# Branch attention with a turned output, a two-unit compressed branch, and two norms merged into one

## The chip, the cores and the metric

The kernel runs on one core of one Trainium2 chip. The metric is the device time of one execution in microseconds (us). Engines: TensorE (PE for its matmuls, PEld for its weight loads), VectorE (DVE), ScalarE (ACT), GpSimd (POOL) and SyncE (SP), which here only issues loads.

## What is computed

Two transformer blocks of two layers each run one after the other on 512 positions of width 1024, in float32. Shown is the second layer of the first block, which the change touches, and the seam to the second block:

```
def nsa_attention(x, norm_g, w_in, w_out, kv):       # 16 heads of 64, 2 key/value groups
    proj = rmsnorm(x, norm_g) @ w_in                  # queries, and a gate per head and branch
    ...
        s = einsum('bghqd,bgnd->bghqn', q_c, k_cmp) * scale          # compressed: 31 keys
        s = jnp.where(valid, s - slopes * dist, NEG)
        p_cmp = softmax(s) * valid.any(-1, keepdims=True)
        o_cmp = einsum('bghqn,bgnd->bghqd', p_cmp, v_cmp)
        ...                                           # o_slc and o_win: the same over the keys up to
        s = jnp.where(ok, s - slopes * dist, NEG)     # the query, with keys and values of their own
        o = g_c[0] * o_cmp + g_c[1] * o_slc + g_c[2] * o_win
    return out @ w_out
...
    return rmsnorm(h, final_norm)                     # end of the first block
    h = rms_norm(x, g_mix[layer])                     # first line of the second
```

With 512 positions the selection takes all 8 blocks and the window spans everything, so both large branches are plain causal attention with a slope per head.

## The kernel before

Activations lie with the width on partitions: `x` is 8 tiles of 128 x 512. A projection splits activations and weights into a high part (fp32r, a rounded float32) and a low rest and takes three fp32r matmuls per pair (`three`). Weights come as panels of 128 x 1024 through a ring of four slots: SP loads `raw`, ACT writes `wh`, DVE writes `wl` (`split_high`, `split_low`, `ahead`), four panels ahead of the matmuls. Results come into four PSUM banks, which DVE empties (`banks_freed`). Each engine runs its instructions in program order; `plan` lists the stages and each stage adds its part to every engine. Semaphores alone tie the engines together.

`Residual` adds a projection to `x`; behind each tile ACT and DVE make the next stage's `xh` and `xl`, and POOL adds the squares into `ssq`. `Norm` turns `ssq` into `rstd`: PE sums over partitions, ACT takes the root, DVE the reciprocal, PE spreads it, DVE copies it out. By default (`late`) PE does this between the panels of the next projection, since the factor is applied to its results; with `now=True` it does it first. At the seam of the blocks a `Norm(now=True)` is followed by `Prepare`, where DVE scales each tile of `x` by the norm and by `final_norm` (L334), ACT and DVE make `xh` and `xl`, and ACT and POOL sum the squares again for a second, late `Norm`.

The attention layer: `KeysValues`, `Project` (queries), `Gates`, `StackQueries` (high and low parts of the queries), `Compress` (the 31 compressed keys and values), `CompressedAttention`, `StackKeys` (keys stacked so that one matmul over 128 rows takes the query's high part against both parts of the key), `CausalAttention("sparse")`, `Split`, and `Residual("w_o")`.

`CompressedAttention` runs 8 units (2 groups x 4 query tiles), each on 128 x 256 scores of 8 heads, in a pipeline over PE (L1453 scores on 64-row tiles, L1462 turning, L1470 values), DVE and ACT, and writes `o` with positions on partitions. `StackKeys` starts when it is over.

`CausalAttention` runs 128 units: 8 head pairs x 2 heads x 2 branches x 4 query tiles. A unit is: two score matmuls of up to 512 columns (L1706, L1707), bias and maximum in one DVE instruction (L1805), exponential with row sum on ACT (L1763), up to four transposes (L1679), a copy to SBUF on ACT (L1752), up to four fp32 matmuls of 128 columns against the values of both groups (L1692), of which one group's 64 columns are used, and on DVE reciprocal, gate and a scaled addition to `o` (L1782, L1823, L1836). Per head ACT also stages bias and queries (L1723, L1731, L1733), `staged_low` with the other head's half set to zero. `Split` then turns `o` into `o_high` and `o_low`.

## Time and profile before

| | |
|---|---|
| median of 3 runs | 2863.46 us (2861.43 to 2864.09) |
| the profiled execution | 2863.38 us, its span 2861.6 us |
| PE / PEld busy | 94% / 77% |
| DVE / ACT / POOL busy | 50% / 35% / 9% |
| mean granted TensorE clock | 0.96 of full speed |

The profiled execution's own time is the span and 1.8 us around it. A matmul's record reaches to its modelled end and overlaps the next one's, so distances between starts tell what a matmul costs, not lengths. The view by stage is that of the busy times in windows.

### The profile page before, as it was taken

How to read it: one execution, taken by the hardware profiler on the slowest of the kernel's cores; microseconds unless marked ns; L12 is line 12 of the kernel's file. 1: busy time of each engine (PE TensorE's matmuls, PEld its weight loads, DVE VectorE, ACT ScalarE, POOL GpSimd, SP SyncE). 2: the span in 40 equal slices, each digit the busy share in tenths (PEclk: the TensorE clock that was granted, in tenths of full speed). 3: DMA queues.
4: the chain of work that ended last, by engine and by line, in shares of the span. 5: the costliest groups of instructions: out<-in, count | busy, mean ns of one | idle time of the engine just before them, and what ended most of it. 6: DMA issues, size and time to landing. Idle time of an engine off the chain costs nothing.

```text
span 2861.6 us, 36729 instructions
## 1 busy us (share of the span) xinstructions
PE 2680.3 (94%) x12628; PEld 2191.1 (77%) x12628; DVE 1438.7 (50%) x2530; ACT 997.2 (35%) x1739; POOL 266.1 (9%) x252
## 2 busy tenths in 40 slices
PE   6989999999788899999799899899999999899999
PEld 5857888878677788888668778688887877588887
DVE  6885444334656554443534455554433565454422
ACT  4544232222377633222232533332322123332321
POOL 2002000110000020002300040200001040200000
PEclk9999999999689999999899999899999998899999
DMA  4202333233200033332222013133322323033331
GB/s 147 67 0 69 101 95 93 80 106 122 70 1 1 0 95 96 95 90 81 86 75 89 1 59 103 30 103 95 93 87 95 104 89 103 30 103 95 93 98 67
DMA packets 61358, 222.45 MB, mean 78 GB/s; under 512 B 7232, under 2 KB 7488, under 8 KB 60624
## 3 DMA queue, kind: packets, MB, share of 16 engines
q1 hardware_dynamic: 58896, 209.15, 23.9%
q0 software_dynamic: 2368, 12.06, 1.3%
q8 instruction: 57, 0.93, 0.1%
q14 instruction: 37, 0.30, 0.0%
HBM read 216.47 MB, written 2.10 MB: 76 GB/s over the span
## 4 chain that ended last, share of the span: by engine, by line
PE 85%; DVE 8%; ACT 3%; issue 2%; DMA 0%; POOL 0%; ACTq 0%; DVEq 0%; SPq 0%; POOLq 0%
PE psum L208 24%; PE psum L209 24%; PE psum L210 24%; PE psum L1692 3%; DVE conv_out L754 2%; PE psum L1679 1%; DVE wl L191 1%; PE psum L1065 1%; PE psum L1117 1%; ACT wh L185 1%; PE psum L1706 1%; PE psum L1707 1%; DVE xl L344 1%; PE psum L1709 1%; PE psum L2313 1%
## 5 line engine op out<-in xcount | busy, mean ns | idle before, releaser
L208 PE MATMUL psum<-xh,wh 128*128 128x512 f32 x1880 | 744.9, 396 | 55.3 <-DVE wl L191 22.9
L209 PE MATMUL psum<-xl,wh 128*128 128x512 f32 x1880 | 739.4, 393 | 0.0
L210 PE MATMUL psum<-xh,wl 128*128 128x512 f32 x1880 | 738.8, 393 | 0.0
L185 ACT ACTIVATE wh<-raw 128x1024 fp32r<-128x1024 f32 x404 | 422.9, 1056 | 895.5 <-PE psum L210 893.1
L191 DVE TENSOR_TENSOR wl<-raw,wh 128x1024 fp32r<-128x1024 f32 x404 | 541.5, 1353 | 246.1 <-ACT wh L185 246.0
L208 PEld LDWEIGHTS psum<-xh,wh 128*128 128x128 f32 x1880 | 356.7, 190 | 139.1 <-issue 27.7
L210 PEld LDWEIGHTS psum<-xh,wl 128*128 128x128 f32 x1880 | 356.5, 190 | 76.4 <-issue 0.9
L209 PEld LDWEIGHTS psum<-xl,wh 128*128 128x128 f32 x1880 | 356.8, 190 | 74.4 <-issue 0.6
L208 PE MATMUL psum<-hidden_high,wh 128*128 128x512 f32 x704 | 278.4, 395 | 0.0
L210 PE MATMUL psum<-hidden_high,wl 128*128 128x512 f32 x704 | 278.0, 395 | 0.0
L209 PE MATMUL psum<-hidden_low,wh 128*128 128x512 f32 x704 | 277.9, 395 | 0.0
L611 POOL TENSOR_TENSOR square<-x 128x512 f32 (+1 forms) x72 | 85.6, 1189 | 1726.5 <-DVE x L650 1509.7
L650 DVE TENSOR_TENSOR x<-psum,x 128x512 f32 (+1 forms) x72 | 49.5, 688 | 324.6 <-PE psum L210 324.5
L503 DVE TENSOR_TENSOR up<-psum,rstd 128x512 f32<-128x512 f32 x96 | 66.3, 691 | 262.6 <-PE psum L210 262.6
L626 ACT ACTIVATE xh<-x,cols (+1 forms) x64 | 46.4, 724 | 363.3 <-DVE x L650 332.8
L208 PEld LDWEIGHTS psum<-hidden_high,wh 128*128 128x128 f32 x704 | 132.3, 188 | 33.7 <-DVE wl L191 2.2
L210 PEld LDWEIGHTS psum<-hidden_high,wl 128*128 128x128 f32 x704 | 132.3, 188 | 31.7
L209 PEld LDWEIGHTS psum<-hidden_low,wh 128*128 128x128 f32 x704 | 132.4, 188 | 31.0
L480 ACT ACTIVATE hidden_high<-up 128x512 f32 x88 | 55.6, 632 | 175.7 <-DVE up L514 175.7
L494 DVE TENSOR_TENSOR pre<-psum,rstd 128x512 f32<-128x512 f32 x96 | 66.3, 691 | 75.7 <-PE psum L210 74.6
L615 POOL TENSOR_TENSOR ssq<-ssq,square 128x512 f32<-128x512 f32 x72 | 103.6, 1438 | 8.0
L518 DVE TENSOR_TENSOR hidden_low<-up,hidden_high 128x512 f32 x88 | 60.9, 692 | 81.8 <-ACT hidden_high L480 81.8
(363 smaller groups left out, 3473.5 us busy)
## 6 DMA issues: line engine op xcount, KB each, us to landing
raw<-ffn_in SPq DMA_DIRECT2D x176, 512.0 KB, 3.5
raw<-ffn_out SPq DMA_DIRECT2D x64, 448.0 KB, 4.1
raw<-ffn_out SPq DMA_DIRECT2D x32, 512.0 KB, 3.6
raw<-pw SPq DMA_DIRECT2D x24, 512.0 KB, 3.6
raw<-o_w_hgg SPq DMA_DIRECT2D x12, 512.0 KB, 4.0
raw<-w_q SPq DMA_DIRECT2D x8, 512.0 KB, 4.3
raw<-w_o SPq DMA_DIRECT2D x8, 512.0 KB, 3.6
raw<-e_w_qk SPq DMA_DIRECT2D x8, 512.0 KB, 3.5
```

The source lines that it names most:

```text
L185: self.nc.scalar.activation(self.wh[:, slot, :], self.raw[:, slot, :], ACT.Copy).then_inc(self.weights_high.sem, 1)
L191: self.nc.vector.tensor_tensor(self.wl[:, slot, :], self.raw[:, slot, :], self.wh[:, slot, :].bitcast(F32), ALU.subtract).then_inc(self.we ...
L208: nc.tensor.matmul(out, ah, bh, start=start, stop=False)
L209: nc.tensor.matmul(out, ah, bl, start=False, stop=False)
L210: return nc.tensor.matmul(out, al, bh, start=False, stop=stop)
L494: dve.tensor_tensor(c.pre[:, r, :], c.psum[:, bank, :], c.rstd[:], ALU.mult).then_inc(c.banks_freed.sem, 1)
L503: dve.tensor_tensor(c.up[:, r, :], c.psum[:, bank, :], c.rstd[:], ALU.mult).then_inc(c.banks_freed.sem, 1)
L518: dve.tensor_tensor(self.hidden[1][:, at, :], c.up[:, r:r + 1, :], self.hidden[0][:, at, :].bitcast(F32), ALU.subtract).then_inc(self.read ...
L611: pool.tensor_tensor(c.square[:, m % 2, :].rearrange("p (a n) -> p a n", a=1), c.x[:, at, :], c.x[:, at, :], ALU.mult).then_inc(self.squar ...
L615: pool.tensor_tensor(c.ssq[:], c.ssq[:], c.square[:, m % 2, :], ALU.add).then_inc(self.summed.sem, 1)
L754: dve.scalar_tensor_tensor(out, taps, w, out, ALU.mult, ALU.add).then_inc(self.tapped.sem, 1)
L1692: mm = pe.matmul(c.psum[:, 1 + u % 2, 0:P], self.pt_sb[u % 4][:, t * P:(t + 1) * P], vals, start=(t == 0), stop=(t == i))
```

## The change

- `CompressedAttention` works in 2 units (one per group) of 128 x 1024: 16 score matmuls each, over all 128 rows against keys laid out in diagonal blocks (`kc` with a column range per half), 4 DVE and 1 ACT instructions over the whole unit, transposes into four banks. It makes no output: its turned probabilities stay as `pt`.
- `StackKeys` moves ahead of `Compress`; its second ACT part (`EvenKeys`) stands behind it.
- `BranchAttention` replaces `CausalAttention("sparse")` and `Split`. A round is one head and one branch with all four query tiles: 32 rounds. Scores: 8 matmuls, of which the four with `low` take only the head's 64 rows. No staging; POOL makes the bias of a head (`slope`). DVE multiplies the probabilities by gate over row sum, in place, in SBUF (L1860 of the changed kernel). Ten transposes fill three and a half banks, one per key tile; DVE copies the widest, ACT the other three. The values are the stationary operand (64 columns), the turned probabilities the moving one (512, 384, 256, 128 columns), and all products of a head pair, the compressed branch's first, add up in one bank that already has the width on partitions; ACT and DVE split it into `o_high` and `o_low` once per pair. `parts[1]` lies over the queries' low part.
- At the seam, `Residual("ffn_out1")` makes `xh` and `xl` with the product of both gains, ACT and POOL sum a second, weighted set of squares beside the first, and `DoubleNorm` works out both norms from them, late. `x` itself is scaled by DVE in `DoubleNorm.vector`, 8 instructions.

```diff
+class DoubleNorm(Norm):
+    def sums(self, pe):
+        pe.wait_ge(s.w_summed.sem, KD + 1)
+        for q, squares in enumerate((c.ssq, c.pre[:, 0, :])):
+            for i in range(NT):
+                mm = pe.matmul(c.psum[:, 5, q * NT + i:q * NT + i + 1], squares[:, i * P:(i + 1) * P],
...
+    def vector(self, dve):
...
+        dve.tensor_copy(c.rstd[:], c.psum[:, 4, :]).then_inc(self.done.sem, 1)
+        for m in range(KD):
+            c.nc.vector.scalar_tensor_tensor(c.x[:, m, :], c.x[:, m, :], c.col("final_norm", m),
+                                             c.psum[:, self.BANK, :], ALU.mult, ALU.mult).then_inc(self.scaled.sem, 1)
+        dve.wait_ge(self.done.sem, self.first + 6)
@@ Residual.gpsimd, Residual.scalar
+                if self.weighted:
+                    pool.wait_ge(self.w_squared.sem, m + 1 + self.body * i)
+                    pool.tensor_tensor(c.pre[:, 0, :], c.pre[:, 0, :], c.up[:, m % 2, :], ALU.add).then_inc(
+                        self.w_summed.sem, 1)
...
+                if self.weighted:
+                    after(act, self.w_summed, m + self.body * i)
+                    act.activation(c.up[:, m % 2, :].rearrange("p (a n) -> p a n", a=1), c.x[:, at, :], ACT.Square,
+                                   scale=c.col("final_norm", m + self.body * i)).then_inc(self.w_squared.sem, 1)
@@ CompressedAttention.tensor
+        for g in range(2):
+            for i in range(NT):
+                for h in range(4):
+                    at = 256 * (i % 2) + 64 * h
+                    mm = pe.matmul(c.psum[:, 2 * g + i // 2, at:at + 64], self.q[:, 4 * g + h, i * P:(i + 1) * P],
+                                   self.comp.kc[:, g, :], start=True, stop=True, skip_group_check=True)
+class BranchAttention(Stage):
+    ROUNDS, SETS, TURNED, RING, BIASES = 4 * KD, 4, 2, 8, 3
+    ORDER, LAID = (3, 2, 0, 1), (0, 1, 3, 2)
+    TURN_LAG, OUT_LAG = 2, 3
+    def tensor(self, pe):
+        for s in range(self.ROUNDS + self.OUT_LAG):
+            if s < self.ROUNDS:
+                self.score(pe, s)
+            if s < 2:
+                self.cmp.turn(pe, s)
+            if 0 <= s - self.TURN_LAG < self.ROUNDS:
+                self.turn(pe, s - self.TURN_LAG)
+            if 0 <= s - self.OUT_LAG:
+                self.weigh(pe, s - self.OUT_LAG)
+    def score(self, pe, n):
+        for i in self.ORDER:
+            if n >= 1 and i != 0:
+                pe.wait_ge(self.scored.sem, self.scored_at(n - 1, {3: 3, 2: 0, 1: 1}[i]))
+            pe.matmul(out, self.stacked.twice[h][:, pair, t], keys[:, 0:width], start=True, stop=False,
+                      skip_group_check=True)
+            mm = pe.matmul(out, self.stacked.low[own, pair, t], keys[own, 0:width], start=False, stop=True,
+                           skip_group_check=True)
+    def weigh(self, pe, n):
+        if n % 4 == 0:
+            pe.matmul(acc, self.comp.vc[:, g, at], self.cmp.pt[:, pair // 2, :], start=True, stop=False,
+                      skip_group_check=True)
+        for t in self.LAID:
+            mm = pe.matmul(acc[own, t * P:S], self.kv.values[:, b, t, 64 * g:64 * g + 64], self.pt[n % self.TURNED][t],
+                           start=False, stop=(n % 4 >= 2 and t == self.LAID[-1]), skip_group_check=True)
+    def vector(self, dve):
+        for s in range(self.ROUNDS + self.OUT_LAG):
+            if s < self.ROUNDS:
+                self.bias_and_max(dve, s)
+            if 0 <= s - 1 < self.ROUNDS:
+                dve.wait_ge(self.probs.sem, 4 * n + 4)
...
+                for i in self.ORDER:
+                    p = self.p[n % self.SETS][i]
+                    dve.tensor_scalar(p, p, self.stat(3, n)[:, i:i + 1], None, ALU.mult).then_inc(self.scaled.sem, 1)
+            n = s - self.TURN_LAG
+            if 0 <= n < self.ROUNDS:
+                dve.tensor_copy(self.pt[n % self.TURNED][0], self.turn_bank(0)).then_inc(self.first.sem, 1)
...
@@ plan
-    norm = add(Norm(c, res, now=True))
-    start = add(Prepare(c, ("g_mix", 0), norm=norm))
-    norm = add(Norm(c, start))
+    res = start = feed_forward("ffn_in1", "ffn_out1", res, norm, ("fn_mix", 0), weighted=True)
+    norm = add(DoubleNorm(c, res))
```

The order of TensorE's instructions in the middle of the old attention, before (one row may stand for several instructions, x is their number; the second name in `psum<-` is the stationary operand):

```order
L1692 MATMUL psum<-values,sparse_pt_124 128x128 x3
L1706 MATMUL psum<-keys_odd,staged_high 128x128
L1707 MATMUL psum<-keys_odd,staged_low 128x128
L1679 MATMUL psum<-ident,sparse_pr_119 128x128 x2
L1692 MATMUL psum<-values,sparse_pt_125 128x128 x4
L1706 MATMUL psum<-keys_odd,staged_high 128x256
L1707 MATMUL psum<-keys_odd,staged_low 128x256
L1679 MATMUL psum<-ident,sparse_pr_120 128x128 x3
L1692 MATMUL psum<-values,sparse_pt_122 128x128
L1706 MATMUL psum<-keys_odd,staged_high 128x384
L1707 MATMUL psum<-keys_odd,staged_low 128x384
L1679 MATMUL psum<-ident,sparse_pr_121 128x128 x4
```

and, after the change, TensorE at the end of one step of `BranchAttention` (the last of four pairs of score matmuls, the transposes of the round two back, the products of the round three back; this step also has the compressed branch's product of its head pair):

```order
L1776 MATMUL psum<-keys_odd,queries_odd 128x256
L1778 MATMUL psum<-keys_odd,queries_low 128x256
L1795 MATMUL psum<-ident,probs_b 128x128
L1795 MATMUL psum<-ident,probs_second_113 128x128
L1795 MATMUL psum<-ident,probs_b 128x128 x2
L1795 MATMUL psum<-ident,probs_second_113 128x128
L1795 MATMUL psum<-ident,probs_b 128x128 x5
L1807 MATMUL psum<-cmp_probs_turned,cmp_values 128x512
L1814 MATMUL psum<-probs_turned_116,values 64x512
L1814 MATMUL psum<-probs_turned_116,values 64x384
L1814 MATMUL psum<-probs_turned_116,values 64x128
L1814 MATMUL psum<-probs_turned_116,values 64x256
```

Unit by unit, with scores, transposes and products in turns, has become round by round: three like pairs of score matmuls stand ahead of these rows, the transposes come in one run, and the products are four wide ones on 64 stationary columns (64 in the row's output shape) instead of ten of 128 columns.

VectorE in the old attention, before:

```order
L1836 SCALAR_TENSOR_TENSOR o<-psum,small,o 128x64
L1782 RECIPROCAL small<-small 128x1
L1804 COPY small<-eps 128x1
L1805 ISA sparse_sc_110,small<-psum,pre 128x128
L1805 ISA small 128x1
L1823 TENSOR_TENSOR small<-small,gates 128x1
L1836 SCALAR_TENSOR_TENSOR o<-psum,small,o 128x64
L1782 RECIPROCAL small<-small 128x1
L1804 COPY small<-eps 128x1
L1805 ISA sparse_sc_111,small<-psum,pre 128x256
```

and VectorE in `BranchAttention`, from the last bias of a round to the first of the next:

```order
L1881 COPY small<-eps 128x1
L1882 ISA probs_second_114,small<-psum,pre 128x256
L1882 ISA small 128x1
L1852 RECIPROCAL small<-small 128x4
L1855 TENSOR_TENSOR small<-small,gates 128x4
L1860 TENSOR_SCALAR probs_b<-probs_b,small 128x512
L1860 TENSOR_SCALAR probs_b<-probs_b,small 128x384
L1860 TENSOR_SCALAR probs_b<-probs_b,small 128x128
L1860 TENSOR_SCALAR probs_second_113<-probs_second_113,small 128x256
L1865 COPY probs_turned_116<-psum 128x512
L1870 TENSOR_TENSOR queries_low<-psum,o_high 128x512
L1881 COPY small<-eps 128x1
```

Two short instructions and a 64-column addition per query tile have become two short instructions per round; four in-place multiplications and a 512-column copy are new, and once per head pair the split of the finished bank (L1870).

TensorE at the seam of the blocks, before:

```order
L96 COMPARE_AND_BRANCH
L377 MATMUL psum<-mean,ssq 128x1 x4
L386 MATMUL psum<-ident,rstd_tok 128x128 x4
L208 MATMUL psum<-xh,wh 128x512
L209 MATMUL psum<-xl,wh 128x512
L210 MATMUL psum<-xh,wl 128x512
```

and after, between the first and second panel of the next projection:

```order
L209 MATMUL psum<-xh,wh 128x512
L210 MATMUL psum<-xl,wh 128x512
L211 MATMUL psum<-xh,wl 128x512
L440 MATMUL psum<-mean,ssq 128x1 x4
L440 MATMUL psum<-mean,pre 128x1 x4
L209 MATMUL psum<-xh,wh 128x512
L210 MATMUL psum<-xl,wh 128x512
```

The sums and the spreading stood between the last matmul of the feed-forward and the projection's first; now the sums (twice as many) stand behind its first panel, and the spreading (L451, also doubled) behind its second.

## Rows read from the trace of the kernel before

**Rows 1.** The page's part 4: share of the chain that ended last, by engine.
```profile
PE 85%; DVE 8%; ACT 3%; issue 2%; DMA 0%; POOL 0%; ACTq 0%; DVEq 0%; SPq 0%; POOLq 0%
```
**Rows 2.** Busy time of each engine in five stretches; columns are in the first line.
```profile
core 0: us, PE busy (x) PEld busy (x) DVE busy (x) ACT busy (x) POOL busy (x), PEclk, DMA share, GB/s
...
742.60:778.30 35.70, 32.10 (x176) 25.46 (x176) 25.73 (x74) 5.75 (x17) 0.00 (x0) 0.54 0.07 26
778.30:787.90 9.60, 0.00 (x0) 0.03 (x1) 5.49 (x8) 7.71 (x12) 0.00 (x0) 0.72 0.00 0
787.90:984.10 196.20, 166.93 (x1216) 151.50 (x1216) 123.49 (x768) 147.07 (x429) 0.00 (x0) 0.95 0.00 1
984.10:991.70 7.60, 4.96 (x32) 3.72 (x33) 3.87 (x6) 3.98 (x7) 0.00 (x0) 0.94 0.00 0
1402.80:1453.50 50.70, 34.76 (x130) 25.89 (x129) 32.75 (x31) 19.56 (x28) 20.46 (x18) 0.73 0.25 75
```
**Rows 3.** Chain of waits, 790 to 984 us: waiter, releaser, total, times, longest.
```profile
DVE small L1804 <- PE psum L1707: 53.8, 74, 3.0
...
PE psum L1706 <- ACT staged_low L1733: 21.1, 14, 2.8
```
**Rows 4.** Timeline of PE and PEld in the old attention: start, length, instructions merged (x).
```profile
904.98 0.60 PE L1679 MATMUL psum<-ident,sparse_pr 128*128 128x128 f32 x4
905.41 0.64 PE L1692 MATMUL psum<-values,sparse_pt 128*128 128x128 f32 x4
...
905.81 0.48 PE L1706 MATMUL psum<-keys_odd,staged_high 128*128 128x512 f32 x1
905.89 0.19 PEld L1707 LDWEIGHTS psum<-keys_odd,staged_low 128*128 128x128 f32 x1
906.13 0.40 PE L1707 MATMUL psum<-keys_odd,staged_low 128*128 128x512 f32 x1
...
906.36 0.27 PE L1679 MATMUL psum<-ident,sparse_pr 128*128 128x128 f32 x1
```
**Rows 5.** Timeline of PE in the memory attention: one 512-column fp32 product, and what follows.
```profile
1801.72 0.59 PE L2313 MATMUL psum<-xa_pt,mv 128*128 128x512 f32 x1
1802.15 0.59 PE L2295 MATMUL psum<-mk,xq 128*128 128x256 f32 x2
```
**Rows 6.** Timeline of PE and PEld, compressed branch: 64-row and 128-row tiles in turn.
```profile
754.21 1.06 PE L1470 MATMUL psum<-cmp_values,cmp_probs_turned 128*128 128x256 f32 x2
...
755.20 1.79 PEld L1453 LDWEIGHTS psum<-cmp_keys,queries 64*128 64x128 f32 x16 [0.65 <-issue]
755.20 1.92 PE L1453 MATMUL psum<-cmp_keys,queries 64*128 64x32 f32 x16
```
**Rows 7.** Groups of DVE by line: busy us, mean ns, idle before.
```profile
L1805 DVE CUSTOM_DVE_ANT_0 sparse_sc<-psum,pre 128x128 f32<-128x128 f32 (+3 forms) x128 | 61.7, 482 | 0.3 <-issue 0.3
...
L2359 DVE TENSOR_SCALAR xa_p<-xa_p,small 128x256 f32<-128x256 f32 x32 | 11.3, 354 | 1.1
...
L406 DVE COPY rstd<-psum 128x512 f32<-128x512 f32 x11 | 7.6, 691 | 69.1 <-PE psum L386 69.1
```
**Rows 8.** Timeline of DVE before the compressed branch, and a group of the key split.
```profile
734.08 4.42 DVE L1562 TENSOR_TENSOR queries_low<-queries,queries_odd 64x4096 f32<-64x4096 f32 x1
...
L1595 DVE TENSOR_TENSOR keys_even<-keys,keys_odd 64x512 fp32r<-64x512 f32 x4 | 2.8, 689 | 0.1
```
**Rows 9.** Timeline of PE: last matmul of a projection, first after the next four.
```profile
1402.56 0.40 PE L210 MATMUL psum<-hidden_high,wl 128*128 128x512 f32 x1
...
1453.49 0.50 PE L208 MATMUL psum<-wh,xh 128*128 128x512 f32 x1 [0.78 <-DVE u L962]
...
2209.96 0.39 PE L210 MATMUL psum<-hidden_high,wl 128*128 128x512 f32 x1
...
2238.47 0.39 PE L208 MATMUL psum<-xh,wh 128*128 128x512 f32 x1
```

More of the change, by code:

```diff
@@ L262, in vector @@
         dve.wait_ge(self.cols_in.sem, 16)
+        cols = self.c.cols
+        fn, mix, both = (slice(AT[n], AT[n] + KD) for n in ("final_norm", "g_mix", "fn_mix"))
+        dve.tensor_tensor(cols[:, both], cols[:, fn], cols[:, mix], ALU.mult).then_inc(self.gains_merged.sem, 1)
     def tensor(self, pe):
@@ L523, with __init__ @@
 class Residual(Stage):
-    def __init__(self, c, weights, act_parts, source, cuts, pack, gain, bias=None, last=False):
+    def __init__(self, c, weights, act_parts, source, cuts, pack, gain, bias=None, last=False, weighted=False):
         self.c, self.weights, self.parts, self.source = c, weights, act_parts, source
+        self.weighted = weighted
         self.cuts, self.pack, self.gain, self.bias, self.last = cuts, pack, gain, bias, last
@@ L1489, in vector @@
+        for k in range(4):
+            act.wait_ge(self.turned.sem, k + 1)
+            act.activation(self.pt[:, k, :], self.c.psum[:, 4 + k, :], ACT.Copy).then_inc(self.copied.sem, 1)
     def vector(self, dve):
@@ L1508, in row @@
-    def row(self, k, u):
-        return self.m[:, 4 * (u % 2) + k, 0:8]
-    def wide(self, k, u):
-        return self.row(k, u).rearrange("p (h a) -> p h a", a=1).to_broadcast([P, 8, 32])
-    def score(self, dve, u):
-        c, (g, i), t = self.c, divmod(u, NT), self.heads(self.t[:, u % 2, :])
-        dve.wait_ge(self.scores.sem, u + 1)
-        after(dve, self.exped, u - 1)
-        for a in range(2):
-            s = c.psum[:, 4 + a + 2 * (u % 2), 0:256].rearrange("p (h n) -> p h n", h=8)[:, a:8:2, :]
-            self.ch.link(dve.tensor_tensor(t[:, a:8:2, :], s, self.bias[:, i, 8 * g + a:8 * g + 8:2, :], ALU.add))
-        self.ch.link(dve.tensor_reduce(self.row(0, u), t, AXX, ALU.max))
-        dve.tensor_tensor(t, t, self.wide(0, u), ALU.subtract).then_inc(self.scored.sem, 1)
@@ L1525, in share @@
-    def share(self, dve, u):
-        c, (g, i), p = self.c, divmod(u, NT), self.heads(self.prob[:, u % 4, :])
-        dve.wait_ge(self.exped.sem, u + 1)
-        self.ch.link(dve.tensor_reduce(self.row(1, u), p, AXX, ALU.add))
-        self.ch.link(dve.reciprocal(self.row(2, u), self.row(1, u)))
-        self.ch.link(dve.tensor_tensor(self.row(3, u), self.row(2, u), self.gates.gates[:, i, 8 * g:8 * g + 8],
+        for g in range(2):
+            self.score(dve, g)
+        for g in range(2):
+            self.share(dve, g)
@@ new lines, in rows, with small, wide, score @@
+    def rows(self, g):
+        return self.t[:, g].rearrange("p i (h n) -> p (i h) n", h=8)
+    def small(self, k, g):
+        return self.m[:, 4 * g + k, :]
+    def wide(self, k, g):
+        return self.small(k, g).rearrange("p (h a) -> p h a", a=1).to_broadcast([P, 32, 32])
+    def score(self, dve, g):
+        c = self.c
+        dve.wait_ge(self.scores.sem, g + 1)
+        self.ch.link(dve.tensor_tensor(self.t[:, g], c.psum[:, 2 * g:2 * g + 2, :].rearrange(
+            "p b (i n) -> p (b i) n", i=2), self.bias[:, :, 8 * g:8 * g + 8, :].rearrange("p i h n -> p i (h n)"),
+            ALU.add))
+        dve.sem_inc(self.added.sem, 1)
+        self.ch.link(dve.tensor_reduce(self.small(0, g), self.rows(g), AXX, ALU.max))
+        dve.tensor_tensor(self.rows(g), self.rows(g), self.wide(0, g), ALU.subtract).then_inc(self.scored.sem, 1)
@@ new lines, in share @@
+    def share(self, dve, g):
+        c = self.c
+        dve.wait_ge(self.exped.sem, g + 1)
+        self.ch.link(dve.tensor_reduce(self.small(1, g), self.rows(g), AXX, ALU.add))
+        self.ch.link(dve.reciprocal(self.small(2, g), self.small(1, g)))
+        self.ch.link(dve.tensor_tensor(self.small(3, g).rearrange("p (i h) -> p i h", i=NT),
+                                       self.small(2, g).rearrange("p (i h) -> p i h", i=NT),
+                                       self.gates.gates[:, :, 8 * g:8 * g + 8], ALU.mult))
+        self.ch.link(dve.tensor_scalar(self.small(3, g)[:, 0:8], self.small(3, g)[:, 0:8], c.col("seen"), None,
@@ L2385, in add, with feed_forward @@
         return stage
-    def feed_forward(w_in, w_out, source, norm, gain, last=False):
+    def feed_forward(w_in, w_out, source, norm, gain, last=False, weighted=False):
         gated = add(Gated(c, w_in, KF, source, norm, hidden=hidden))
-        return add(Residual(c, w_out, hidden, From(gated.ready, gated.ready0), [7, 7, 8], 1, gain, last=last))
+        return add(Residual(c, w_out, hidden, From(gated.ready, gated.ready0), [7, 7, 8], 1, gain, last=last,
+                            weighted=weighted))
     def memory_attention(layer, free, w_out, mixer_parts, source):
@@ L2453, in plan @@
     comp.gates = gates
+    keys = add(StackKeys(c, kv, gates))
     add(comp)
+    add(EvenKeys(keys))
     cmp_att = add(CompressedAttention(c, q, kv, comp, gates, qp))
@@ L2460, in plan @@
     dist = add(Loads(c, [(distance[:], c.dram["distance"])], gates_done, "distance_in"))
[L2462 to L2481 removed]
+    att = add(BranchAttention(c, stacked, keys, kv, comp, cmp_att, gates, distance, dist))
+    parts = att.parts
+    res = add(Residual(c, "w_o", parts, From(att.ready, att.ready0), [KD], 1, ("ffn_norm", KD)))
     norm = add(Norm(c, res))
[L2483 to L2488 removed]
+    res = start = feed_forward("ffn_in1", "ffn_out1", res, norm, ("fn_mix", 0), weighted=True)
+    norm = add(DoubleNorm(c, res))
     parts = (c.arena("ey_high", 0, [P, KD, S], FR), c.arena("ey_low", 16, [P, KD, S], FR))
```

336 lines of the change are left out of this document (238 added, 98 removed).

## Prediction

> **What bounds the kernel now.** The chain that ended last is TensorE for 85% [rows 1], so only what shortens TensorE's stretches or its waits counts. Read the busy times by stage next [rows 2]: the old attention takes 196.2 us with TensorE busy for 166.9, the compressed branch 35.7 at a granted clock of 0.54 (1.2 GHz nearly throughout), the key split 9.6 with TensorE idle, `Split` 7.6, and the seam from the last feed-forward matmul to the first of `e_w_v` 50.7 at a clock of 0.73. In the attention TensorE waited 21.1 us for the staged queries, 14 times, about once a head [rows 3]; VectorE waited 53.8 us for scores, so it has room.
>
> **The steady round.** The old kernel spends 196.2 / 32 = 6.13 us per head and branch. What TensorE does in one, at 2.4 GHz: a score matmul of 512 columns costs 0.23 (906.13 to 906.36), so 2 x 1280 columns cost 1.15; four transposes cost 0.43, ten 1.08 [rows 4]. An fp32 instruction of 512 columns costs 0.43 and a product takes two [rows 5], so 1280 columns cost 2.15; the ten narrow products of before stream the same 1280 columns. To this comes the compressed product, 0.86 per four rounds, 0.21. Sum 4.6 us, and nothing in it got smaller: what the new form removes is the staging wait (1.3 us per head) and the per-unit turns.
>
> What it adds is a change of tile shape inside the scores. `low` now takes 64 rows, `twice` 128, and they alternate. In rows of one shape, the load for L1707 starts at 905.89, 0.24 us ahead of its matmul, under L1706; also L1706 itself takes 0.32 instead of 0.23 behind an fp32 product [rows 4]. Where 128-row and 64-row tiles meet, nothing is loaded ahead: two instructions of 0.43 from 754.21 on end at 755.07, the load starts at 755.20, and the matmul no earlier, with no wait between ("issue") [rows 6]. That is a pause of 0.13 at half clock, and behind it a load that is no longer hidden. The load's length I take from the same place: the 16 fp32 matmuls of 32 columns, in pairs, last 1.92, so 0.21 to 0.24 per pair, set by loads; half of that, 0.11, at full clock, as the four transposes also show (0.43 / 4, equal for load and stream). A switch inside the scores then costs 0.09 + 0.11 = 0.20 (bounds: 0.09, if the load could be had for nothing, and 0.27, if the pause is 0.13 at any clock and the stream starts late). Seven in the scores make 1.4, the step to the transposes 0.09, to the products and back 0.1. **Round: 4.6 + 1.6 = 6.2 us**, bounds 5.4 and 6.7.
>
> The Trainium skill (TensorEngine Tiling (Array Packing), section Key Properties) says that changing the tiling mode, and not just the tile, drains TensorE; the trace agrees, with the 0.13 of [rows 6]. The Trainium skill's page TensorE: Matmul & The Clock Gate, section Single matmul latency, gives (398 + N) / 2.4 ns for a single matmul at full clock, 166 ns over its columns; an estimate with eight switches at that price is a round of 6.0 and a total of 2818 us. Priced by the rows of one shape alone, with no charge for a switch, TensorE's round would be 4.7, and rival 1 would come true.
>
> **The other engines in a round.** VectorE: four bias-and-maximum instructions 4 x 0.48 = 1.93 [rows 7]. In the old attention it was busy 123.5 / 32 = 3.86 per round [rows 2]; the other 1.93 are 20 short ones, 0.1 each. Now 8 such (0.8), two that wait for each other (0.5), four multiplications from SBUF to SBUF, nearest 0.35 for 256 columns, so 4 x 0.39 at most and 1.3 with their overlap, one copy of 0.69, and the pair's split 0.69 / 4 [rows 7]. 5.2 us, 5.7 with nothing overlapped: below 6.2, above 4.9. So VectorE is no bound at my price, and sets the floor of 5.2 if switches are free. ScalarE was busy 147.1 / 32 = 4.6 with four copies and the staging; it loses the staging and the widest copy, so it stays below. POOL's 16 biases have three buffers; it is idle otherwise.
>
> Does a wait close the round? A round's scores wait for VectorE's maxima of the round before, its transposes for the scaling done one step earlier, its products for copies of one step earlier. Scaling ends about 4.9 after a step's start and is needed at 6.2 + 2.6. Once per pair VectorE waits for ScalarE's half of the finished bank (0.7 behind TensorE's step) and loses under 1 us, of which the next step gives 1 back. Hidden, as long as the round stays above 5.7.
>
> **The front.** `StackKeys` now stands before `Compress` on VectorE. The queries' low parts end at 738.5; eight subtractions of 0.69 follow, to 744.0 [rows 8], then 12 small copies instead of 10. The scores, which began at 742.6 [rows 2], begin at about 746.7: 4 us lost here, and 9.6 of the key split with its wait saved behind. Compressed scores: 32 instructions per group on full tiles, bound by loads of 0.21 at half clock [rows 6], 6.8 us per group, to 760.3, against 8 units of 16 matmuls before: no gain. VectorE needs three passes of 1024 columns (4096 took 4.42 on the same engine [rows 8], so 1.1, with waits 1.25) per group before the exponentials and two with small ones between behind them, in the order score, score, share, share: done at 770.6. TensorE makes the first round's scores from 761.7. But its second round waits for VectorE (771.3), runs at 1.2 GHz (4.9 us), and only then come the second group's transposes, the last two copies, and, behind them on ScalarE, the first exponential: 778.5. First scaling done 782.5, first real transposes there. All rounds but three scores of 2.7 us are still to come: attention ends at 782.5 - 8 + 32 x round = **774.5 + 32 x round**. With 6.2: 972.9. `w_o` starts at once, as seven of its eight inputs are long ready and the eighth has 4.8 us; it began at 991.7 before. **Saved: 18.8 us**, of it 7.6 from `Split`. The steady part itself gives almost nothing: 6.2 against 6.13.
>
> **The seam.** A like seam without a norm in the way is there already: 2209.96 to 2238.47, 28.5 us over four panels, against 1402.56 to 1453.49, 50.9 [rows 9]. On top of 28.5 come four more sums and four more spreadings (0.9 each) and, in front of the evictions, 8 scalings of `x` at 0.69, 5.5 us. In the like seam VectorE has about 4 us of room before the fifth panel needs the banks, so 1.7 of these show. 28.5 + 1.8 + 1.7 = 32.0: **saved 18.9**. The added squares on ScalarE and sums on POOL lie under 15 us of matmuls per tile; POOL's last sum comes at about 1410, when the sums are due. Bounds: 13, if both are late by a few us, and 22.
>
> The first matmuls of `w_o` no longer run at half clock: 1 us. Sum: 18.8 + 18.9 + 1 = 38.7. Against the profiled execution (2863.4, span 2861.6, as good as the median 2863.5): **2824 us**.
>
> **The rivals.**
> 1. Switches cheap (0.05 or less): VectorE's 5.2 bounds the round. Attention ends at 940.9, and with the seam the time is 2863.4 - 50.8 - 19.9 = 2793. For it: at full clock no switch is on record here. Against: [rows 6] shows a load that starts only after the pause. Chance 0.14.
> 2. VectorE late: its waits on itself and on ScalarE add 0.15 at each of 12 places to 5.7, round 7.0: attention at 998.5, time 2863.4 + 6.8 - 19.9 = 2850. For it: 5.7 without overlap. Against: it had 53.8 us of waiting for TensorE [rows 3]. Chance 0.08.
> 3. The merged norm gives under 8 us since scaling `x` holds back evictions and POOL is late: about 2836. Chance 0.08.
> 4. Slower than before: a switch at full clock costs so much that the attention eats the seam's gain too. That needs 774.5 + 32 x round above 991.7 + 19.9, a round above 7.4, or 0.37 us per switch, over all rows here. At 0.40 it would be 2870. Chance 0.04.
> My forecast, a round of 5.4 to 6.7 and a seam of 13 to 22, has 0.66 and on its own gives 2799 to 2841.
>
> **How the numbers follow.** The likeliest case gives 2824. Rival 1 reaches down to 2793, and I stop at 2794; at the top 2842 takes in rival 3 and leaves out 2 and 4. A measurement of this kernel tells 0.2% (5.7 us) from no change. Rivals 2 and 4 and the rare sum of two bad bounds give the chances: faster 0.93, within 0.2% 0.03, slower 0.04.
>
> **What would show it.** In the changed kernel: score matmuls of `low` whose load does not start before the matmul ahead has drained, 0.2 us dearer each way; rounds of 6.2 us; no idle time of TensorE for staging; VectorE near 5 us busy per round; `w_o` beginning near 973; `e_w_v` about 32 us behind the last feed-forward matmul. Wrong if loads run ahead across shapes (then rival 1), or if TensorE stands idle for scaling in every round (rival 2).

## The result, and the profile after

| | before | after |
|---|---|---|
| median | 2863.78 us (2861.43 to 2867.63, 4 runs) | 2844.89 us (2842.65 to 2846.87, 4 runs) |
| span profiled, mean clock | 2861.6 us, 0.960 | 2842.2 us, 0.965 |

The ratio is 0.9933, 95% interval 0.9919 to 0.9947: 19 us faster, where 38.7 were forecast; the time lies 2.9 us above the range.

Where the 19.4 us between the two spans come from is read off the starts of five matmuls of TensorE. "Gates" is the first matmul of the compressed hidden product behind the gates (726.52 before, 728.16 after):

| stretch | before | after | gain | forecast |
|---|---|---|---|---|
| start to gates | 726.5 | 728.2 | -1.6 | 0 |
| gates to the first matmul of `w_o` | 265.2 | 258.1 | 7.1 | 18.8 |
| `w_o` to the end of `ffn_out1` | 410.9 | 410.6 | 0.3 | 1 |
| the seam, to the first matmul of `e_w_v`'s product | 50.9 | 34.8 | 16.2 | 18.9 |
| from there to the last matmul of the last hidden product | 1401.1 | 1403.3 | -2.2 | 0 |

What stands behind that matmul, 7.0 us before and 7.3 after, brings the sum to 19.4, up to rounding.

The page's part 4 after:

```profile
PE 87%; DVE 8%; ACT 2%; issue 1%; DMA 0%; DVEq 0%; ACTq 0%; POOL 0%; SPq 0%
```

TensorE has an even larger share of the chain than in [rows 1]. The windows of the changed kernel (columns in the first line), the stages of [rows 2]:

```profile
core 0: us, PE busy (x) PEld busy (x) DVE busy (x) ACT busy (x) POOL busy (x), PEclk, DMA share, GB/s
...
748.80:764.20 15.40, 13.91 (x64) 13.75 (x65) 4.94 (x5) 1.06 (x1) 4.52 (x3) 0.50 0.00 0
764.20:789.50 25.30, 20.12 (x52) 12.52 (x52) 17.42 (x58) 11.55 (x31) 1.08 (x1) 0.50 0.00 1
789.50:986.30 196.80, 196.80 (x814) 108.48 (x814) 136.43 (x570) 99.68 (x335) 22.29 (x14) 1.00 0.00 1
```

The last row tells most. The new attention keeps TensorE busy without a gap, at full clock, and lasts 196.8 us; the old one took 196.2 with 166.9 busy. What the staging waits gave was spent on matmuls that cost more. From the gates to these stretches it took 61.3 us after and 61.4 before, so the front gave nothing either. `Split`'s 7.6 us are gone: the 7.1 of the table. VectorE was busy 136.4 us, 4.5 per round of 6.48, and ScalarE 99.7; neither bounds. One round on TensorE, timeline of PE's weight loads (start, length, "idle before"):

```profile
899.84 0.19 PEld L1776 LDWEIGHTS psum<-keys_even,queries_even 128*128 128x128 f32 x1 [0.39 <-issue]
900.27 0.18 PEld L1778 LDWEIGHTS psum<-keys_even,queries_low 64*128 64x128 f32 x1 [0.24 <-issue]
900.69 0.19 PEld L1776 LDWEIGHTS psum<-keys_even,queries_even 128*128 128x128 f32 x1 [0.24 <-issue]
901.06 0.18 PEld L1778 LDWEIGHTS psum<-keys_even,queries_low 64*128 64x128 f32 x1 [0.18 <-issue]
...
902.25 0.18 PEld L1778 LDWEIGHTS psum<-keys_even,queries_low 64*128 64x128 f32 x1
902.56 0.14 PEld L1795 LDWEIGHTS psum<-ident,probs_c 128*128 128x128 f32 x1
```

and PE's matmuls beside them:

```profile
899.84 0.49 PE L1776 MATMUL psum<-keys_even,queries_even 128*128 128x512 f32 x1
900.27 0.49 PE L1778 MATMUL psum<-keys_even,queries_low 64*128 64x512 f32 x1
900.69 0.44 PE L1776 MATMUL psum<-keys_even,queries_even 128*128 128x384 f32 x1
901.06 0.44 PE L1778 MATMUL psum<-keys_even,queries_low 64*128 64x384 f32 x1
...
902.57 0.33 PE L1795 MATMUL psum<-ident,probs_c 128*128 128x128 f32 x1
903.81 2.37 PE L1814 MATMUL psum<-probs_turned,values 128*64 128x512 f32 x8
906.11 0.50 PE L1776 MATMUL psum<-keys_odd,queries_odd 128*128 128x512 f32 x1
```

Each load starts with its own matmul, not ahead of it as in [rows 4], and 512 columns take 0.43 us instead of 0.23. The scores last 2.73 us (899.84 to 902.57), the transposes 1.24, the products 2.30: 6.27, and 0.21 of compressed product makes 6.48.

### The profile page after: what moved, and what is told of

Same layout as the page of the kernel before. It is cut to its first block, busy times and chain, and to the rows that moved or that the text cites. A ratio compares the mean times of both kernels' runs of the same rounds, so it can differ in the third digit from the quotient of the medians.

```text
span 2842.2 us, 34266 instructions
## 1 busy us (share of the span) xinstructions
PE 2706.4 (95%) x12132; PEld 2146.5 (76%) x12132; DVE 1429.2 (50%) x2317; ACT 947.8 (33%) x1649; POOL 287.2 (10%) x268
## 4 chain that ended last, share of the span: by engine, by line
PE 87%; DVE 8%; ACT 2%; issue 1%; DMA 0%; DVEq 0%; ACTq 0%; POOL 0%; SPq 0%
PE psum L209 24%; PE psum L210 24%; PE psum L211 24%; PE psum L1814 3%; DVE conv_out L844 2%; PE psum L1776 1%; PE psum L1778 1%; PE psum L1795 1%; DVE wl L192 1%; PE psum L1207 1%; PE psum L1155 1%; ACT wh L186 1%; PE psum L1997 1%; PE psum L2601 1%; DVE xl L745 1%
## 5 line engine op out<-in xcount | busy, mean ns | idle before, releaser
L192 DVE TENSOR_TENSOR wl<-raw,wh 128x1024 fp32r<-128x1024 f32 x404 | 533.0, 1332 | 262.3 <-ACT wh L186 262.3
L710 ACT ACTIVATE xh<-x,cols (+1 forms) x72 | 52.2, 724 | 456.4 <-DVE x L740 425.6
L690 POOL TENSOR_TENSOR square<-x 128x512 f32 (+1 forms) x72 | 78.4, 1089 | 1243.2 <-DVE x L740 1026.0
```

Of the source, the lines that this page charges most:

```text
L192: self.nc.vector.tensor_tensor(self.wl[:, slot, :], self.raw[:, slot, :], self.wh[:, slot, :].bitcast(F32), ALU.subtract).then_inc(self.we ...
L690: pool.tensor_tensor(c.square[:, m % 2, :].rearrange("p (a n) -> p a n", a=1), c.x[:, at, :], c.x[:, at, :], ALU.mult).then_inc(self.squar ...
```

## The experiments

The figures per kernel are medians; "before" was timed again with each group (2862.1 to 2865.0), and the ratios go by that. A meeting is a place in TensorE's order where a matmul on 128 rows and one on 64 rows stand side by side.

### Where the round's time is: e1, e2, e3

```diff
-        for i in self.ORDER:                      # twice, low, twice, low, ...
-            pe.matmul(out, self.stacked.twice[h][:, pair, t], keys[:, 0:width], ...)
-            mm = pe.matmul(out, self.stacked.low[own, pair, t], keys[own, 0:width], ...)
+        for tiles in ((3, 2, 0, 1),):             # e2_pairs: ((3, 2), (0, 1))
+            for i in tiles:
+                pe.matmul(self.score_bank(i), self.stacked.twice[h][:, pair, i * P:(i + 1) * P], ...,
+                          start=(i != 0), ...)    # tiles 2 and 0 share a bank
+            for i in tiles:
+                mm = pe.matmul(self.score_bank(i), self.stacked.low[own, pair, i * P:(i + 1) * P], ...)
```

**e1_grouped.** 

> Edit on the changed kernel: in a round all four score matmuls of `twice` (128 rows) first, then all four of `low` (64 rows), so that the shape changes once inside the scores and once behind them, not seven times and once. Same sums and same columns. Theory (each meeting of a 128-row and a 64-row tile costs 0.20 us): six meetings fewer, the round falls from 6.27 to 5.07 us (compressed product not counted), about 29 rounds, so 2844.9 - 34 = 2811 us. Rival A (the cost sits in every 64-row matmul, wherever it stands, as a dearer load): nothing changes, 2845. Rival B (VectorE, busy 4.4 to 4.7 us per round, and its waits become the bound near 5.5): 2823.

**e2_pairs.** 

> Edit on the changed kernel: scores in two groups, `twice` of tiles 3 and 2, `low` of 3 and 2, then the same for 0 and 1, so four meetings of shapes fewer in a round instead of six. Theory: the round falls by 0.8 to 5.47 us, 2844.9 - 23 = 2822 us, two thirds of what full grouping gives. Rival A: 2845. Rival B (VectorE near 5.5): the same time as full grouping, 2823.

**e3_full_rows** (`low[:, pair, t]` against `keys[:, 0:width]`). 

> Edit on the changed kernel: the matmuls of `low` take all 128 rows of both operands, in the old order, so no shape changes in the scores; this adds the other head's low part to each score, so the output is another one and only the time counts. Theory: all eight meetings gone, TensorE's own round 4.67 us; VectorE, busy 4.4 to 4.7, is then as late as TensorE, so the round is 4.7 to 5.0 and the time 2844.9 - 29 x 1.4 = 2804 us (2799 to 2809). Rival A gives the same here as the theory; the two are told apart by the grouped order. If the cost is in neither (each matmul of a pair simply takes long), 2845.

| | median | ratio, 95% interval | round | meetings fewer | us per meeting |
|---|---|---|---|---|---|
| changed kernel | 2844.89 | 0.9933 (0.9919 to 0.9947) | 6.27 | | |
| e1_grouped | 2812.85 | 0.9818 (0.9802 to 0.9835) | 5.21 | 6 | 0.177 |
| e2_pairs | 2822.10 | 0.9853 (0.9837 to 0.9870) | 5.59 | 4 | 0.17 |
| e3_full_rows | 2801.97 | 0.9784 (0.9768 to 0.9800) | 4.86 | 8 | 0.176 |

The round is the distance from one round's first transpose to the next one's, without the compressed product. Three doses give one price. Rival A falls with e1, where the same 64-row matmuls stand in another order; rival B with all three, since TensorE had no idle time even in rounds of 4.86 us, and VectorE waited for it. Grouping also pulls apart the two matmuls that add up in one place of a bank, but that isn't the cause: e3 leaves them side by side, in the old order, and gains the most. The scores of e1_grouped on PE:

```profile
875.37 0.91 PE L1776 MATMUL psum<-keys_odd,queries_odd 128*128 128x512 f32 x4
876.21 0.91 PE L1779 MATMUL psum<-keys_odd,queries_low 64*128 64x512 f32 x4
877.04 0.33 PE L1796 MATMUL psum<-ident,probs_b 128*128 128x128 f32 x1
```

Four `twice` take 0.84 us and four `low` 0.83, against 2.73 for the eight in turn. VectorE's waits in e3_full_rows, 800 to 930 us (waiter, releaser, total, times, longest):

```profile
DVE small L1881 <- PE psum L1778: 12.4, 19, 1.1
```

It still waits for TensorE (before: 53.8 us, [rows 3]), so it has room at 4.86 us per round.

### The two parts alone: e4, e5

**e4_seam_only.** 

> The kernel before with the merged norm alone (`DoubleNorm`, weighted squares and sums, gains merged), the attention as it was. From the trace of after the seam between the last matmul of the hidden product and the first of `e_w_v` with its wait went from 50.9 to 34.8 us. Theory: the seam is a matter of its own and gives 16 us here too, 2863.8 - 16 = 2848 us (ratio 0.9944). Rival (the seam's gain hangs on the attention's buffers or is given back by the later stages, where the trace of after lost 2.5 us): under 14, 2850 or more.

**e5_attention_only.** 

> The changed kernel with the old end of the feed-forward block (two norms, no merged one), so the new branch attention alone. From the trace of after `w_o` begins 5.5 us earlier and its first matmuls run 0.7 us faster. Theory: 6 us, 2863.8 - 6 = 2858 us (ratio 0.998); the two parts add up to the whole, 19 to 22 us. Rival (attention gives what the forecast said, 20, and the whole lost it elsewhere): 2844.

e4: 2852.15 us (2843.91 to 2853.93, 5 runs), ratio 0.9963 (0.9950 to 0.9976), 11 us. e5: 2859.68 us (2856.09 to 2867.80, 12 runs), ratio 0.9992 (0.9981 to 1.0002), 3 us, not told from none. By the traces the seam is 34.0 us in e4 and 51.2 in e5, and the gates come 258.6 us ahead of `w_o` in e5 (265.2 before): the same stretches as in the whole. The medians add up to 14 and the whole is 19, within intervals of 4 us on each. The expectation of e4 (2848) is missed by 4. Its trace is that of its fastest run, 2843.91 us at a mean granted clock of 0.966; the other four took 2852 to 2854 at 0.962 to 0.964, and where they lost it no trace shows. So the stretches of e4 are not those of its median. The new attention is 6.6 us shorter in e5's trace, but its medians can't tell it from no change; most of this kernel's gain is the seam's.

### The front: e6, e7

e6 moves VectorE's key subtractions (`StackKeys.vector`) into `EvenKeys`, so behind `Compress`; e7:

```diff
-            if s < 2:
-                self.cmp.turn(pe, s)
+            if s == 0:
+                self.cmp.turn(pe, 0)
+                self.cmp.turn(pe, 1)
```

**e6_keys_late.** 

> Edit on the changed kernel: VectorE's eight key subtractions (5.7 us) stand behind the copies of `Compress` instead of ahead of them, so that they lie in the 7.3 us in which VectorE waits for the first compressed scores. Theory: the copies end at 745.2 instead of 748.8, the compressed scores begin 3.6 us earlier and so does all behind them: 2841.3 us against 2844.9 (ratio to before 0.992). Rival (the chain of the second round's scores, the second group's transposes and ScalarE's first exponential takes it up): under 1 us.

**e7_turn_early.** 

> Edit on the changed kernel: the transposes of the second compressed group stand ahead of the second round's scores, not behind them. Theory (the first exponential waits on ScalarE behind the copies of these transposes, which wait on TensorE behind a round of scores at 1.2 GHz): copies done at 776.5 instead of 781.1, first exponential 4.6 us earlier, first real transposes behind the third round's scores at about 784.3 instead of 786.6: 2.3 us, 2842.6 us. Rival (VectorE's late scores of the second round close the gap again): 0 to 1 us, 2844 to 2845.

What both aim at, VectorE's timeline of the changed kernel:

```profile
740.18 0.68 DVE L1662 TENSOR_TENSOR keys_odd<-keys,keys_odd 64x512 fp32r<-64x512 f32 x1
...
745.92 0.84 DVE L1418 COPY cmp_keys<-psum 64x31 f32<-64x31 f32 x4
746.79 1.98 DVE L1423 COPY cmp_values<-psum 31x64 f32<-31x64 f32 x8
756.05 1.22 DVE L1584 TENSOR_TENSOR cmp_scores<-psum,cmp_bias 128x1024 f32<-128x1024 f32 x1 [7.28 <-PE psum L1540]
```

and ScalarE's, ahead of the first exponential (L1825):

```profile
780.52 0.60 ACT L1560 ACTIVATE cmp_probs_turned<-psum 128x512 f32<-128x512 f32 x1 [0.26 <-PE psum L1549]
781.14 1.28 ACT L1819 ACT_TABLE_LOAD   x1
782.43 0.72 ACT L1825 ACTIVATE probs_a<-probs_a,small 128x512 f32<-128x512 f32 x1
```

e6: 2843.46 us, ratio 0.9931 (0.9918 to 0.9943). Its gates come as late as in the changed kernel (728.25) and `w_o` 3.1 us earlier (983.17): the theory holds in the trace (3.6 were expected); the medians cannot tell 1.4 from 3. e7: 2841.94 us, ratio 0.9928 (0.9915 to 0.9940); gates to `w_o` 257.8 for 258.1. Against its own gates the first real transposes came 2.9 us earlier, but the clock did not. Windows of e7:

```profile
780.00:785.00 5.00, 5.00 (x17) 3.74 (x16) 4.17 (x18) 3.34 (x11) 1.76 (x1) 0.50 0.00 0
785.00:790.00 5.00, 5.00 (x15) 3.28 (x15) 3.20 (x16) 2.40 (x8) 0.86 (x1) 0.50 0.00 0
790.00:791.00 1.00, 1.00 (x5) 0.96 (x5) 1.00 (x4) 0.56 (x3) 0.89 (x1) 0.54 0.00 0
```

TensorE, busy without a gap, did these rounds at 1.2 GHz until after 790, where the changed kernel had full clock from 789.5 on.

### Where the rest was lost: e8

Every kernel with the merged norm has hidden products of 528 matmuls that last 123.4 to 123.5 us, in the first block too, ahead of any change; before and in e5 they last 122.7 to 123.0.

```diff
-        self.cols = self.place("cols", [P, NCOLS + KD])
+        self.cols = self.place("cols", [P, NCOLS + 2 * KD])
```

**e8_aligned.** 

> Edit on the changed kernel: one tile, `cols`, is allocated 8 columns wider and nothing else. The change itself made it 32 bytes longer, which moved all that lies behind it in SBUF, `hidden` among it, from a multiple of 64 bytes to 32 behind one; 8 more columns bring it back. In the traces the four hidden products of 528 matmuls last 123.4 to 123.5 us in every kernel with the longer `cols` and 122.7 to 123.0 in the two without. Theory (the address is the cause): 122.8 to 123.0 here, four times 0.5 and a little elsewhere, 2 to 3 us in all, 2842.5 us. Rival (the straightened loops of the merged norm, or chance, are the cause): 123.5 as before and 2845 us.

2840.20 us (2838.26 to 2843.84), ratio 0.9922 (0.9908 to 0.9935), which alone can't be told from the changed kernel's 0.9933. The four products last 123.2, 123.0, 123.1 and 123.0, in all 1.7 us less. A group of these matmuls in part 5 of the page (busy, mean ns), changed kernel:

```profile
L210 PE MATMUL psum<-hidden_low,wh 128*128 128x512 f32 x704 | 279.0, 396 | 0.0
```

e8_aligned:

```profile
L210 PE MATMUL psum<-hidden_low,wh 128*128 128x512 f32 x704 | 277.7, 395 | 0.0
```

The theory holds for these products: it is 32 bytes of place, since e8 keeps the merged norm's code. The first of them is still 0.3 us longer than before and in e5, and why is open.

The last stretch of the table falls by 2.5 us in e8 (1400.8 for 1403.3), but only 0.9 of that lies in the two products behind the seam. Another 1.7 lies between the first matmul on `xo` in the last memory attention and the first of the feed-forward behind it. That stretch (columns as in the windows above), in this order, in the kernel before, the changed one, e4, e8 and e13:

```profile
2456.33:2503.07 46.74, 40.96 (x163) 32.27 (x161) 20.87 (x22) 14.06 (x17) 19.56 (x16) 0.87 0.15 46
2436.14:2482.89 46.75, 41.10 (x162) 32.25 (x161) 20.87 (x22) 14.07 (x17) 19.58 (x16) 0.87 0.15 45
2437.98:2483.11 45.13, 39.51 (x163) 31.23 (x161) 20.87 (x22) 14.07 (x17) 19.57 (x16) 0.89 0.16 47
2434.50:2479.55 45.05, 39.36 (x162) 31.13 (x161) 20.85 (x22) 14.07 (x17) 19.55 (x16) 0.89 0.16 47
2395.28:2442.30 47.02, 41.35 (x162) 32.34 (x161) 20.85 (x22) 14.06 (x17) 19.55 (x16) 0.86 0.14 45
```

Its length goes with the granted clock (0.86 to 0.87 or 0.89) and not with the place of `hidden`: e4 has the place of the changed kernel and is short, the kernel before and e13 have `hidden` on a multiple of 64 bytes and are long. What decides the clock there these runs don't tell.

### Together: e9, e10, e12

**e9_combined.** 

> The changed kernel with scores grouped as in e1_grouped, key subtractions behind the copies as in e6_keys_late, and `cols` widened as in e8_aligned. Theory (independent effects, each as its trace showed: 31.4 us up to the start of `w_o`, 3.1 us, 2.2 us): the stretch from the gates to `w_o` is 226.8 - 3.2 = 223.6 us and the time 2812.9 - 5.3 = 2807.5 us. Rival (an earlier start at 1.2 GHz gives the clock back later, so the 3 us of the keys vanish): 2810.5 us.

**e10_combined_turn.** 

> As e9_combined, and the second compressed group's transposes ahead of the second round's scores, as in e7_turn_early, where the first real transposes came 2.9 us earlier, the clock rose no earlier, and 0.3 us were left at `w_o`. Theory (TensorE only moves work into the stretch at 1.2 GHz): the same as e9_combined within 1 us, 2807.5. Rival (with shorter rounds the 2.9 us are kept): 2804.5 us.

e9: 2806.85 us (2806.16 to 2808.20), ratio 0.9806 (0.9793 to 0.9819); gates to `w_o` 225.1 us. e10: 2801.82 us (2800.86 to 2803.08), ratio 0.9788 (0.9775 to 0.9801); 221.3 us. e9's time came as expected (the stretch 1.5 us longer), e10 did not: the turn placed early comes with 5 us here, 3.8 of them between gates and `w_o`; another 1.5 stand ahead of the gates, where the two kernels are the same, and can't be put down to it. Windows of e10:

```profile
775.00:780.00 5.00, 5.00 (x20) 4.35 (x20) 4.93 (x23) 3.93 (x15) 1.76 (x1) 0.50 0.00 0
780.00:785.00 5.00, 5.00 (x17) 3.17 (x16) 4.46 (x19) 3.09 (x11) 1.75 (x1) 0.62 0.00 0
785.00:790.00 5.00, 5.00 (x27) 3.33 (x26) 2.04 (x13) 1.23 (x4) 0.00 (x0) 1.00 0.00 0
```

Here the clock rose at about 784, not behind 790: whether an earlier start is kept hangs on when the clock rises. Why it rose earlier here than in e7 these runs don't tell.

**e12_combined_turn_again.** 

> The kernel of e10_combined_turn once more, on the same chip as e11_square_late, so that a difference of a us or two can be told. Both theories: 2801.8 us within 1.5, seam 34.8 us.

2801.82 us again (2800.29 to 2803.21), ratio 0.9787 (0.9773 to 0.9800): 61 us faster than before and 43 than the changed kernel, with nothing left out.

### The seam: e11, e13

```diff
+                for j in self.panels_of(m):
+                    c.ahead(c.split_high, act, self.panel0, j, i, self.body_panels)
                 if self.weighted:
                     after(act, self.w_summed, m + self.body * i)
                     act.activation(c.up[:, m % 2, :]..., c.x[:, at, :], ACT.Square, ...)
-                for j in self.panels_of(m):
-                    c.ahead(c.split_high, act, self.panel0, j, i, self.body_panels)
```

**e11_square_late.** 

> Edit on e10_combined_turn: ScalarE's weighted square of each output tile stands behind the tile's three panel splits, not ahead of them. In the seam it delays the splits by 0.6 us on ScalarE, VectorE's three splits take 4.6 instead of 4.0 us, and the last low part of `x`, for which TensorE waits, comes 1.0 us later than in the like seam. Theory (this delay is the first part of the 2.8 us by which the seam missed its forecast, the other part being sums at 1.2 GHz behind the longer pause): the wait falls from 3.8 to 2.8 us and the seam from 34.8 to 33.8 us, 32.5 if the sums also come at full clock; 2801.8 - 1 to 2 = 2800 us. Rival (the square, now 2.9 us later, makes POOL's last weighted sum late and the sums wait for it): seam 35 us or more, 2802 us or more.

2802.25 us (2800.91 to 2803.29), ratio 0.9789 (0.9776 to 0.9802); seam 34.9 us, 35.1 in e12. The wait stayed at 3.8 us and the theory fell: the splits took 5.2 us, and now the third, beside POOL's weighted sum, was the long one (2.3 us), while the first, beside POOL's other sum, took 1.9. e13 in POOL's part:

```diff
-                    pool.tensor_tensor(c.pre[:, 0, :], c.pre[:, 0, :], c.up[:, m % 2, :], ALU.add)...
+                    n = S if m + self.body * i < KD - 1 else 1
+                    pool.tensor_tensor(c.pre[:, 0, 0:n], c.pre[:, 0, 0:n], c.up[:, m % 2, 0:n], ALU.add)...
```

**e13_no_last_sum.** 

> Edit on e10_combined_turn: POOL's weighted sum of the last output tile covers 1 column instead of 512, so that the weighted norm leaves out 511 columns of one tile of eight; the output is another one, only the time counts. In the seam one of VectorE's three splits lasts 2.29 us where it overlaps this sum (2.26 us) and 1.21 to 1.29 where it overlaps none, in e11_square_late too, where square and sum came later and the slow split with them. Theory (VectorE's split waits while POOL's sum runs): the three splits take 3.6 to 3.8 us in place of 4.7, the wait for the last low part falls from 3.8 to 2.7 us and the seam from 34.8 to 33.8, to 32.5 if the pause is then short enough that the sums come at full clock. Time 2799 to 2801 us. Rival (the long split has another cause, the DMA issues or ScalarE's table load): seam stays at 34.8 to 35.1.

VectorE's three splits, POOL's sum and the wait that ends with them, changed kernel:

```profile
1400.44 4.63 DVE L192 TENSOR_TENSOR wl<-raw,wh 128x1024 fp32r<-128x1024 f32 x3 [2.35 <-ACT wh L186]
1400.60 2.26 POOL L698 TENSOR_TENSOR pre<-pre,up 128x512 f32<-128x512 f32 x1
1405.79 0.79 PE L209 MATMUL psum<-xh,wh 128*128 128x512 f32 x1 [3.77 <-DVE xl L745]
1406.38 0.63 PE L210 MATMUL psum<-xl,wh 128*128 128x512 f32 x1
```

e13_no_last_sum:

```profile
1360.00 3.56 DVE L192 TENSOR_TENSOR wl<-raw,wh 128x1024 fp32r<-128x1024 f32 x3 [2.36 <-ACT wh L186]
1360.15 1.18 POOL L699 TENSOR_TENSOR pre<-pre,up 128x1 f32<-128x1 f32 x1
1364.27 0.79 PE L209 MATMUL psum<-xh,wh 128*128 128x512 f32 x1 [2.69 <-DVE xl L746]
```

The splits fall from 4.63 to 3.56 us and the wait by 1.1, as expected; the seam falls to 34.2, not to 33.8, since what follows still ran at 1.2 GHz (the panel behind the sums took 7.8 us for e10's 7.3). The time, 2803.91 us (2802.94 to 2806.17), ratio 0.9793 (0.9777 to 0.9809), shows no gain: behind the seam that profile took 3 us more (1403.3 for e10's 1400.2), 1.9 of them in the stretch shown under e8 (47.0 for 45.1). So e13 shows what holds the split, by its trace alone. The Trainium skill (SBUF — State Buffer, section SBUF: two separate sides) has VectorE and GpSimd take turns at a shared pair of ports, whole instructions at a time, when VectorE's instruction has two inputs in SBUF and GpSimd's reads SBUF. The trace agrees: a split of 1.21 becomes 2.29 beside a sum of 2.26, and the sum of one column in e13 lasts 1.18, until the split that was running is done.

## Why the prediction was wrong

**The step that failed is "Round: 4.6 + 1.6 = 6.2 us"** and with it "attention ends at 774.5 + 32 x round". The mechanism and, within 0.03 us, the price of a switch were right; the sizes of small terms were not, and 32 rounds multiply them. Measured is 6.48, so 0.28 x 32 = 9.0 us of the 20 that are missing. Its terms follow from the distances between starts in e3_full_rows, where no meeting is left and a round is 4.86 without the compressed product, against 4.4 of streams and 0.1 for the way to the products and back:

```profile
874.98 0.71 PE L1795 MATMUL psum<-ident,probs_c 128*128 128x128 f32 x5
875.62 2.37 PE L1814 MATMUL psum<-probs_turned,values 128*64 128x512 f32 x8
877.91 0.50 PE L1776 MATMUL psum<-keys_odd,queries_odd 128*128 128x512 f32 x1
878.25 0.39 PE L1778 MATMUL psum<-keys_odd,queries_low 128*128 128x512 f32 x1
...
878.83 0.22 PE L1776 MATMUL psum<-keys_odd,queries_odd 128*128 128x128 f32 x1
878.89 0.27 PE L1778 MATMUL psum<-keys_odd,queries_low 128*128 128x128 f32 x1
879.00 0.33 PE L1776 MATMUL psum<-keys_odd,queries_odd 128*128 128x256 f32 x1
879.17 0.28 PE L1778 MATMUL psum<-keys_odd,queries_low 128*128 128x256 f32 x1
879.29 0.28 PE L1795 MATMUL psum<-ident,probs_d 128*128 128x128 f32 x1
```

- The switches: eight at 0.176 (e3), 1.40; forecast seven at 0.20 and one at 0.09, 1.49. This term was 0.09 too dear.
- "To the products and back 0.1": with the tiles of 64 columns the last transpose takes 0.20 for 0.11, the first product 0.48 for 0.43, the last 0.31 for 0.22, the next score 0.34 for 0.23, in all 0.35, so 0.25 too little. In the rows of before, where all products have 128 columns, going there and back cost 0.04 in all, so the change to 64 columns is the likely cause; no run changed it alone.
- "2 x 1280 columns cost 1.15": 1.27 without that. Two scores of 128 columns take 0.17 for 0.12 and two of 256 take 0.29 for 0.23: 0.12 too little. That a short matmul doesn't hide the next load fits this, but no run tried it.

**The front, "first real transposes there" (782.5): 786.6**, another 4.1 us. 1.6 were there ahead of the gates: 0.6 is the first block's hidden product (e8 gives back 0.3 of it), the other 1.0 came before and behind it, and the gates' start varies from profile to profile, 725.2 to 728.4. VectorE was done with the shares at 773.2 for 770.6, of which 1.6 are the gates again, and one step was left out: the exponential's table load of 1.28 us on ScalarE behind the last two copies. That the key subtractions cost what they showed was right, and avoidable (e6).

**The seam: 34.8 for 32.0**, a gain of 16.2, inside its bounds of 13 to 22. The 144 matmuls behind the norm took 34.2 us, and 34.0 before, so the scalings of `x` stayed hidden, for which 1.7 were forecast, and the sixteen matmuls of the spreadings took 1.7 for 0.8 with eight, as priced. Not foreseen: POOL's weighted sum holds a split of VectorE (1 us, shown by e13), and behind the longer pause the clock was at 1.2 GHz, so that the sixteen matmuls of the sums took 3.3 us where the like seam's eight took 0.8 to 0.9; that step was priced at full clock. The three matmuls ahead of them lost 0.6 in the same way. And the like seam was too short a model: from the last spreading to `e_w_v` it takes 11.0 us, this seam 11.9 before the change and 12.1 after.

**At no price**, the prediction took all that it did not name, and there 2.2 us were lost: 1.3 in the two hidden products, of which 0.9 are the 32 bytes by which `cols` grew (e8), and 0.9 at places for which there is no experiment.

**The rivals.** 1 is out: a switch costs 0.176. Its floor was wrong too: the prediction's terms for VectorE add up to 5.4 us, not to 5.2, and VectorE was busy 4.6 per round in the changed kernel and 4.3 in e3, whose rounds of 5.07 with the compressed product stayed below that floor. 2 is out: VectorE never held a round, even of 4.86 (and 5.7 with 12 times 0.15 would have been 7.5, not 7.0). 3 is out (16 us). 4, at 0.37 per switch, was twice the truth. None had the combination that came: round and seam in their bounds, both on the dear side, and a late front that had no bounds. The two bad bounds together (6.7 and 13) give 2847 by the prediction's own sum, so the range up to 2842 was cut narrower than what it was made of. Right were `Split`'s 7.6 us, TensorE without idle time, and that the steady part gives nothing. The direction, with 0.93 for faster, was right by the seam: the attention, from which half of the gain was to come, is not told from no change by itself (e5). Two sums are slips that decide nothing: 2863.4 less 38.7 is 2824.7, and 5.5 us of scalings less 4 of room are 1.5, not 1.7.

## What to carry to other kernels

Order matmuls by tile shape: every place where 128-row and 64-row tiles meet cost 0.176 us at full clock, and eight of them in a round of 6.3 us cost more than what the new form had saved; grouping them gave back 32 us with the same products added up. Price a round of short matmuls by what a like row of that width takes behind another, loads and column shapes included, since an error of 0.28 us is 9 us after 32 rounds. An instruction that is hidden on its own engine can still hold another: POOL's sum doubled a split of VectorE that TensorE waited for.

## What was not expected of the hardware

- fp32r matmuls of 512 columns (528 in a row) followed each other every 0.2342 to 0.2344 us with `hidden` at byte 136736 of a partition, 32 off a multiple of 64, and every 0.2333 to 0.2337 with it at 136768 (e8); at 136704, before, it was 0.2328 to 0.2333. Over this kernel e8 gained 1.7 us by it. Other places, and which of `hidden`'s two parts it is, were not tried.
- A meeting of tile shapes cost 0.176 us at full clock and 0.27 to 0.30 at 1.2 GHz: in the first round's scores of the changed kernel 512 columns took 0.70 us (764.20 to 764.90), and 0.43 where the shape stays.
- TensorE, busy without a gap at 1.2 GHz from 775 on, got full clock at about 784 in e10 and after 790 in e7, in almost the same program.
